# Seven block products in place of eight at 31 places of the down products, and a ring of eight weight slots in place of ten

## What is computed

```python
def second_block(x, attn_norm, w_in, ..., w_o, mlp_norm, w_up, w_down, final_norm):
    for l in range(DEPTH):
        h = rms_norm_2(x, attn_norm[l])
        proj = h @ w_in[l]
        ...
        x = x + mixed @ w_o[l]
        h = rms_norm_2(x, mlp_norm[l])
        x = x + jnp.square(jax.nn.relu(h @ w_up[l])) @ w_down[l]
    return rms_norm_2(x, final_norm)
```

## Time and profile before

| | |
|---|---|
| runs | 2908.87, 2910.0 and 5743.55 us, median 2910.0 |
| profiled execution, time | 2908.11 us |
| its span | 2906.3 us |
| mean granted TensorE clock | 0.994 |
| TensorE busy with matmuls | 2826.6 us, 14616 matmuls |
| VectorE busy | 1895.0 us |
| ScalarE busy | 1439.6 us |
| moved by DMA | 611.88 MB, mean 211 GB/s |

### The profile page before, as it was taken

One profiled execution on the slowest core, in us unless ns is written; L12 is line 12 of the kernel. 1 busy time (PEld: TensorE's weight loads), 2 busy tenths in 40 slices (PEclk: granted clock), 3 DMA queues, 4 the chain that ended last, 5 costly groups with the idle time before them and its releaser, 6 DMA issues.

```text
span 2906.3 us, 36886 instructions
## 1 busy us (share of the span) xinstructions
PE 2826.6 (97%) x14616; PEld 2440.8 (84%) x14616; DVE 1895.0 (65%) x2401; ACT 1439.6 (50%) x2029; POOL 39.0 (1%) x48
## 2 busy tenths in 40 slices
PE   5998998999999999999999999999999999999998
PEld 5887787898889888888888888898888888888887
DVE  7999998679854566655445554545666654456554
ACT  5455544565546554644334444555546443344443
POOL 0000000000000000000000000000000000000000
PEclk9999999999999999999999999999999999999999
DMA  9996598767655455556665566564545556655653
GB/s 392 363 361 225 195 370 301 248 201 259 240 170 185 150 174 163 177 189 191 194 194 188 189 192 193 180 186 153 171 164 176 191 191 195 193 186 191 206 195 138
DMA packets 173882, 611.88 MB, mean 211 GB/s; under 512 B 19680, under 2 KB 19952, under 8 KB 173072
## 3 DMA queue, kind: packets, MB, share of 16 engines
q1 hardware_dynamic: 170912, 600.42, 61.4%
q0 software_dynamic: 1824, 6.61, 0.8%
q10 hardware_dynamic: 976, 2.51, 0.3%
HBM read 607.34 MB, written 2.11 MB: 210 GB/s over the span
## 4 chain that ended last, share of the span: by engine, by line
PE 86%; DVE 7%; ACT 2%; DMA 2%; issue 1%; SPq 0%; POOL 0%; POOLq 0%; ACTq 0%; DVEq 0%
PE ps L2025 19%; PE ps L2028 19%; PE ps L2032 18%; PE ps L2044 16%; PE ps L2054 8%; DVE w_lo L1260 2%; PE ps L1971 2%; DVE raw L1416 2%; PE ps L2252 1%; DMA raw<-in_w_ina 1%; PE ps L2231 1%; ACT w_hi L883 1%; DMA raw<-in_w_modT 1%; DVE proj L1390 1%; DMA raw<-in_w_in 0%
## 5 line engine op out<-in xcount | busy, mean ns | idle before, releaser
L1260 DVE TENSOR_TENSOR w_lo<-raw,w_hi 128x1024 fp32r<-128x1024 f32 (+4 forms) x988 | 1149.8, 1175 | 865.1 <-ACT w_hi L883 862.0
L883 ACT ACTIVATE w_hi<-raw 128x1024 fp32r<-128x1024 f32 (+4 forms) x988 | 994.5, 1018 | 1168.7 <-PE ps L2032 642.9
L2025 PE MATMUL ps<-w_hi,hT_both 128*128 128x512 f32 (+3 forms) x1824 | 478.9, 384 | 15.9 <-DVE proj L1390 8.1
L2044 PE MATMUL ps<-hT_both,w_hi 128*128 128x512 f32 x2048 | 490.2, 391 | 0.9 <-DVE u L1364 0.9
L2028 PE MATMUL ps<-w_lo,hT_both 128*128 128x512 f32 (+3 forms) x1824 | 462.2, 375 | 0.6 <-DVE w_lo L1260 0.6
L2032 PE MATMUL ps<-w_hi,hT_both 128*128 128x512 f32 (+3 forms) x1824 | 459.3, 373 | 0.0
L2044 PEld LDWEIGHTS ps<-hT_both,w_hi 128*128 128x128 f32 x2048 | 376.1, 188 | 74.1 <-DVE u L1364 1.3
L2028 PEld LDWEIGHTS ps<-w_lo,hT_both 128*128 128x128 f32 x1824 | 339.7, 189 | 50.8 <-DVE w_lo L1260 1.9
L2025 PEld LDWEIGHTS ps<-w_hi,hT_both 128*128 128x128 f32 x1824 | 326.9, 189 | 63.0 <-DVE proj L1390 12.2
L2032 PEld LDWEIGHTS ps<-w_hi,hT_both 128*128 128x128 f32 x1824 | 339.1, 188 | 48.4
L2025 PE MATMUL ps<-w_hi,uT_hi 128*128 128x512 f32 x1024 | 275.1, 390 | 0.0
(11 more groups left out here) (256 smaller groups left out, 1549.7 us busy)
## 6 DMA issues: line engine op xcount, KB each, us to landing
raw<-in_w_up SPq DMA_DIRECT2D x256, 512.0 KB, 3.8
raw<-in_w_down SPq DMA_DIRECT2D x256, 512.0 KB, 4.2
raw<-in_w_modT SPq DMA_DIRECT2D x192, 512.0 KB, 5.8
raw<-in_w_rest SPq DMA_DIRECT2D x80, 456.0 KB, 3.5
raw<-in_w_z SPq DMA_DIRECT2D x64, 512.0 KB, 4.4
raw<-in_w_out SPq DMA_DIRECT2D x64, 512.0 KB, 4.4
raw<-in_w_rest SPq DMA_DIRECT2D x48, 344.0 KB, 3.4
raw<-in_w_oa SPq DMA_DIRECT2D x32, 512.0 KB, 3.4
```

What stands on the lines that cost most here:

```text
L883: act.activation(hi_blocks(L % SPLIT_SLOTS, c, w), blocks(raw, G % RAW_SLOTS, c, w), ACT.Copy).then_inc(S.hi_ready, 1)
L1260: dve.tensor_tensor(blocks(w_lo, r, c, w), blocks(raw, r, c, w), hi_blocks(s, c, w).bitcast(F32), ALU.subtract).then_inc(S.group_read, 1)
L2025: pe.matmul(o, rows(hi, c, t), wh[:, c], start=start and c == 0, stop=False)
L2044: pe.matmul(ps[:, bank(job, i, f)], wh[:, c, f * P:(f + 1) * P], hT_both[:, k0 + c].rearrange("p a n -> p (a n)"), start=k0 + c == 0, stop ...
```

## The change

A pair of column tiles of a down job is now taken together (`joined` pairs of tiles: two in down00, down01 and down10, one in down11), with the steps of the two tiles alternating. At the groups in `QUADS` (2, 5, 8, 11 for the first half, 2, 4, 6, 8, 10 for the second) the two groups hold a matrix of 2 x 2 weight blocks (two chunks, two tiles), and u holds 2 x 2 blocks (two tokens' blocks, two chunks). Their product is made with seven block products and not eight, after Winograd's form of Strassen's scheme. It needs four sums of left blocks, made and split when the up tile is (`sums`), and three combinations of right blocks, made from the raw weights (`combine`, then `combos_hi` and `combos_lo`). Three of the seven go to three of the four banks of the pair's tiles (`c11`, `c12`, `c21` in the code), four to banks 4 to 7, where they add up over the quads of a pair; `take_parts` then adds them to x. There are 8 + 10 + 8 + 5 = 31 such quads. TensorE does nothing in the first step of a quad and 21 matmuls in the second.

The ring has eight slots and not ten; its place is used for the sums and combinations. The turned blocks for `c21` come at other steps, and the final norm's row is loaded later, since the tiles that they need end in another order.

```diff
-RAW_SLOTS = 10
+RAW_SLOTS = 8
+QUADS = ((2, 5, 8, 11), (2, 4, 6, 8, 10))
...
     def steps(self):
         tiles, groups = range(self.tiles), range(len(self.groups))
+        if self.joined:
+            return ([(2 * p + a, j) for p in range(self.joined) for j in groups for a in range(2)]
+                    + [(i, j) for i in tiles[2 * self.joined:] for j in groups])
...
-                    product(f"down{l}{h}", (uT_hi, uT_lo), evac="dve", tail=TAIL if l == DEPTH - 1 and h else 0))])]
+                    product(f"down{l}{h}", (uT_hi, uT_lo), evac="dve", tail=TAIL if l == DEPTH - 1 and h else 0,
+                            joined=1 if l == DEPTH - 1 and h else 2, quads=QUADS[h]))])]
...
-        lead("c21", *after("c21", -8, -7, -6, -5, -4, -3, 3, 4))
+        lead("c21", *after("c21", -4, -3, -2, -1, 1, 2, 3, 4))
...
-            pool.wait_ge(S.group_multiplied, jobs["down11"].L)
+            pool.wait_ge(S.group_multiplied, jobs["down11"].L + 2 * len(jobs["down11"].groups))
...
+                if job.seven(i, j) and i % 2:
+                    act.wait_ge(S.combined, 4 * quad_of(i, L) + 2)
                 act.wait_ge(raw_landed[G % RAW_SLOTS], 16 * (G // RAW_SLOTS + 1))
...
+                    act.activation(combos_hi[h][:], combos[h][:], ACT.Copy).then_inc(S.combos_rounded, 1)
...
+            def combine(job, i, L):
+                h, q = int(job.name[-1]), quad_of(i, L)
+                e = combos[h]
+                first, second = (blocks(raw, group_at[L + a] % RAW_SLOTS, 2, COLS) for a in range(2))
+                b11, b21, b12, b22 = first[:, 0], first[:, 1], second[:, 0], second[:, 1]
...
+                if q:
+                    dve.wait_ge(S.combos_multiplied, q)
...
+                dve.tensor_tensor(e[:, 0], b22, b12, ALU.subtract).then_inc(S.combined, 1)
...
+                dve.tensor_tensor(b12, b12, b11, ALU.subtract).then_inc(S.combined, 1)
...
+                dve.tensor_tensor(e[:, 1], b22, b12, ALU.subtract).then_inc(S.combined, 1)
...
+                dve.tensor_tensor(e[:, 2], b21, e[:, 1], ALU.subtract).then_inc(S.combined, 1)
...
+                a11, a12, a21, a22 = v[:, 0, 0:P], v[:, 1, 0:P], v[:, 0, P:2 * P], v[:, 1, P:2 * P]
+                dve.tensor_tensor(to[:, 2], a11, a21, ALU.subtract).then_inc(S.sums_ready, 1)
+                dve.tensor_tensor(to[:, 0], a21, a22, ALU.add).then_inc(S.sums_ready, 1)
...
+                dve.tensor_tensor(to[:, 1], to[:, 0], a11, ALU.subtract).then_inc(S.sums_ready, 1)
...
+                dve.tensor_tensor(to[:, 3], a12, to[:, 1], ALU.subtract).then_inc(S.sums_ready, 1)
...
+            def seven_products(job, p, j, L):
...
+                plain = [(ps[:, 4], left(0, 0), hi0[:, 0], lo0[:, 0], True), (c11, left(1, 0), hi0[:, 1], lo0[:, 1], False),
+                         (c12, total(3), hi1[:, 1], lo1[:, 1], False), (ps[:, 5], total(0), hi1[:, 0], lo1[:, 0], True)]
+                mixed = [(o, a, combos_hi[h][:, k], combos_lo[h][:, k], own)
+                         for k, (o, a, own) in enumerate(((ps[:, 7], total(2), True), (ps[:, 6], total(1), True), (c21, left(1, 1), False)))]
...
+                mm.then_inc(S.group_multiplied, 2)
+                pe.wait_ge(S.combos_rounded, q + 1)
...
+                pe.wait_ge(S.combos_split, q + 1)
...
+                mm.then_inc(S.combos_multiplied, 1)
```

More of the change, by code:

```diff
@@ L206, in steps, with together, seven, after_quads @@
         return [(i, j) for j in groups for i in tiles] if self.swept else [(i, j) for i in tiles for j in groups]
+    def together(self, i):
+        return i < 2 * self.joined
+    def seven(self, i, j):
+        return self.together(i) and j in self.quads
+    def after_quads(self, i, j):
+        return 2 * (j - max(self.quads) - 1) + i % 2 if self.together(i) else -1
     def in_tail(self, i, j):
@@ L559, in up_tiles, with quad_of, last_quad, sums_of @@
             return ups.index(job) * job.tiles + i + 1
+        downs = [jobs[f"down{l}{h}"] for l in range(DEPTH) for h in range(2)]
+        summed = {(job.layer, int(job.name[-1]), j): k
+                  for k, (job, j) in enumerate((job, j) for job in downs for j in job.quads)}
+        quad_at = {L: k for k, L in enumerate(L for job in downs for q, (i, j) in enumerate(job.steps())
+                                              for L in (job.L + q,) if i % 2 and job.seven(i, j))}
+        superpairs = {(job.name, p): k for k, (job, p) in enumerate((job, p) for job in downs for p in range(job.joined))}
+        def quad_of(i, L):
+            return quad_at[L if i % 2 else L + 1]
+        def last_quad(job, p):
+            return quad_at[job.L + job.steps().index((2 * p + 1, max(job.quads)))]
+        def sums_of(job, i):
+            down = jobs["down" + job.name[-2:]]
+            return down.quads.index(i) if i in down.quads else None
         def ahead(jobs_):
@@ L566, in ahead @@
                 end = min(q + AHEAD + 1, len(groups))
-                yield (*group, [(job, j, L) for job, i, j, L in groups[upto:end]])
+                yield (*group, groups[upto:end])
                 upto = end
@@ L1070, in wide @@
                         out_squares(job, i - 1)
-                    if i and j == 3 and job.kind == "down" and job.name[-1] == "1":
-                        squares_of(job, i - 1, junk_m[:])
+                    if job.joined and job.after_quads(i, j) == 1:
+                        copy_part(job, i // 2)
+                    if i >= 2 and i % 2 == 0 and j == 3 and job.name == "down01":
+                        for done in range(2):
+                            squares_of(job, done, junk_m[:])
+                    if i >= 2 and j == 3 and job.name == "down11":
+                        for done in range(2) if i == 2 else (2,):
+                            squares_of(job, done, junk_m[:])
                     if j == last:
@@ L1223, in _ @@
                 else:
-                    squares_of(jobs[f"down{l - 1}1"], 3, probs2[:, 0])
+                    for done in (2, 3):
+                        squares_of(jobs[f"down{l - 1}1"], done, probs2[:, 0])
                 walk.upto(c2.L + 18)
@@ L1254, in link, with lo @@
                 dve.wait_ge(S.dve_step, n(S.dve_step))
-            def lo(job, j, L):
+            def lo(job, i, j, L):
+                if job.seven(i, j) and i % 2 == 0:
+                    combine(job, i, L)
                 dve.wait_ge(S.hi_ready, L + 1)
@@ L1391, in evacuate @@
                     return
+                if job.kind == "down" and job.together(i):
+                    dve.wait_ge(S.part_added, 4 * (superpairs[job.name, i // 2] + 1))
                 for t in range(TOK):
@@ L1455, in wide @@
                 prev = None
+                ended = []
                 for job, i, j, L, splits in ahead(order):
@@ L1458, in wide @@
                         tail(job, j - len(job.groups) + TOK)
+                    if ended and ended[0][2] <= L:
+                        evacuate(*ended.pop(0)[0:2])
                     if prev and prev[0].kind in ("inb", "inc", "ind") and j == 1:
```

142 lines of the change are left out of this document (137 added, 5 removed).

## The result

The changed kernel takes 2940.3 us (2938.64 to 2944.43), the kernel before in the same comparison 2909.43 us. The ratio is 1.0111, with a 95% interval from 1.0094 to 1.0129. So it is 31 us slower, where 6 us faster was forecast, and outside the range of 2889 to 2917. That is under 2%, but the interval lies wholly above 1. The profiled execution took 2939.47 us. One profiled execution of a later kernel (z0's loads spread evenly at ten slots) took 3081.2 us at a mean granted clock of 0.865, where its other four took 2895 to 2897, and no reading rests on it.

A forecast was written before the change was run, and what follows sets the result against it. TensorE's matmuls plus its pauses were taken to bound the kernel. 2908.1 - 21.1 (matmuls) + 2.6 (bank waits) + 12.7 (fewer slots) = 2902.3 us; with 1.9 from profiled execution to median, 2904 us, range 2889 to 2917.

The forecast's parts named there:

- A saved matmul: Down products: each of 93 matmuls saved was to be worth its pitch of 0.2267 us, together 21.1 us.
- the fourth rival: Matmuls saved in the down products are worth only 131 ns each, giving 2913 us; chance 0.02.
- The wait of a down product's second group: Each of four down products: TensorE waits 0.65 us for VectorE to finish with a bank, +2.6 us in all.
- The combinations are hidden: Dense quads: VectorE's combinations fit behind 10.2 us of matmuls, 0.65 and 1.4 us to spare, cost 0 us.
- The third rival: Combinations come late in the dense quads, 1 us of wait at twelve quads, giving 2916 us; chance 0.08.
- the next tile finds its bank drained: End of a pair in down products: evacuation takes 1.5 us, TensorE's group between 2.72, so no wait was expected.
- the sum's ring term: First network's four stretches: eight load slots for ten were to cost 12.7 us in all.
- z0.: Stretch z0: loads for steps 6 to 13 wait for the product three groups back, +2.5 us (0 to 28).
- in1.: Stretch in1: later loads for groups 7, 10, 13 and 16 were to cost +7.7 us (3 to 11).
- ina to ind.: Stretch ina to ind: one group later, +2.44 us, mostly cancelled by shorter queueing, -2.6; +2 us taken (0 to 41).
- The second rival: Fewer slots cost more than the saved matmuls give, mainly in z0 and ina to ind: 2921 us; chance 0.18.
- The first rival: Fewer slots cost nothing, since queueing shrinks by just what is lost: 2891.5 us; chance 0.2.

## Why the prediction was wrong

**What held.** A saved matmul is worth 0.2267 us and the down products are TensorE's throughout (24 matmuls again: +21.1), so the fourth rival is out. The wait of a down product's second group for the bank that `square_u` drains came as forecast, in one place per job:

```profile
1403.54 1.07 PE L2205 MATMUL ps<-w_hi,uT_lo 128*128 128x512 f32 x4
1405.11 1.20 PE L2198 MATMUL ps<-w_hi,uT_hi 128*128 128x512 f32 x4 [0.50 <-DVE u L1503]
```

The packs of four are spaced 0.91 us, so the product before ended at 1404.45 and the pause is 0.66 us, for 0.65 forecast. The combinations are hidden. At a dense quad of down01 (VectorE, then TensorE):

```profile
1788.67 0.69 DVE L1373 TENSOR_TENSOR combos<-raw,combos 128x512 f32<-128x512 f32 x1
...
1791.68 1.75 DVE L1352 TENSOR_TENSOR combos_lo<-combos,combos_hi 128x1536 fp32r<-128x1536 f32 x1
...
1794.97 0.61 PE L2251 MATMUL ps<-combos_lo,sums_hi 128*128 128x512 f32 x2
```

Their low part is ready at 1793.43, 1.5 us ahead of its matmul; 1.4 was the forecast. The third rival is out. The 1.8 us that the down products gave less lie mostly at the end of down01, where c21's first group finds its bank occupied. The prediction had priced this at nothing ("the next tile finds its bank drained"):

```profile
1920.62 1.09 PE L2198 MATMUL ps<-w_hi,hT_both 128*128 128x456 f32 x4 [1.10 <-DVE x L1496]
```

A joined pair ends both tiles together, so the last but one is drained later than when tiles ended sixteen groups apart.

**The step that failed** is the sum's ring term, 12.7 us for a measured 47.8, and within it three sentences.

*z0.* "But a group's product comes two long steps after its split, and VectorE has other work: of 0 to 9 x 3.1 = 28 us I take +2.5." It cost 16.2. The prediction followed the late load to its own product, which does come two steps later, and gave it that slack. But ScalarE and VectorE work through their lists in order. The rounding and the split that wait for the load stand ahead of attention work for an earlier step, and the product just before needs that. The loop is product L - 3, load L, product L - 1. The turn shown above takes 12.0 us and brings two products, 6.0 us each; with the release four back the same turn would bring three, 4.0 us each. Measured over those eight steps are 7.2 us a step at three back (changed kernel), 5.3 at four (kernel before), 5.0 at four to five (spread evenly, eight slots). In pairs, as a turn brings them, steps 7 to 14 took 12.0, 12.5, 13.6 and 19.7 us, for 9.4, 10.7, 10.7 and 11.6 before. So every turn loses, as the distance of the release has it, but over half of the loss in these steps is in the last, at step 13. There the load of step 15, released by the product of step 12, holds the list of ScalarE ahead of attention work (`probsT`):

```profile
303.56 5.38 DMA raw<-in_w_z
...
309.93 0.59 ACT probsT L1172
...
310.56 3.67 PE ps L2475 x16
```

TensorE stood still for 6.2 us (0.7 at the same place before), and the sixteen matmuls behind that took 3.67 us for 2.00. The rule of one turn gives the direction of the loss and not its size.

*in1.* The sum there was 2.7 and 2.2 us for two loads and 1.4 each for two others, 7.7 us. The loop was seen, the load of group 10 was issued at 525.31 with the product of group 7 as forecast, and the sign was right. The size was 19.4, and two causes can be named. The first is the start. In the kernel before, the load of group 5 was issued at 454.23, ahead of TensorE's long pause before in1, and in the changed kernel it waits out the pause:

```profile
483.95 16.90 SPq L860 DMA_DIRECT2D raw<-in_w_modT  x2
503.24 0.33 SPq L860 DMA_DIRECT2D raw<-in_w_in  x1
```

It lands at 506.77, and group 6 then comes 8.0 us after group 5, 5.2 more than its own length. The rows are SyncE's; the first covers two `W_mod` loads, the second of which went out behind the pause. In the plan the release of group 5's load moves across the pause, from out0's last product to in1's second, and the prediction looked at groups 7, 10, 13 and 16 only. The run with 14 `W_mod` loads in in1 has this release back at out0's last product and all the later ones four or more back; in1 was 22 us shorter in it. Group 6 still took 5.2 us there, so the release of group 5's load is not shown to be the whole of its growth. The second cause is the later pauses. The groups behind one, 9, 12 and 15, took 7.6, 10.1 and 8.3 us for 4.7, 4.6 and 6.5 before, and group 18, for which the sum had nothing, took 6.3 for 2.7. Part of both is that TensorE ran slower behind the pauses, for which the sum had no term either: by the busy times above that is 6.9 of the 19.4 us. Group 9 grew by 2.9 us for 2.7 forecast, and that is luck. The load of 4.75 us in the earlier trace rows was not without a queue ahead, as the prediction has it: two `W_mod` loads issued at 486.19 were still under way. In the changed kernel it took 3.52 us, 1.2 less, and twelve matmuls behind the pause that took 4.26 us in place of 2.72 took this back.

*ina to ind.* "Most of it cancels": two loads fewer in the queue were to give back 2.6 us of 2.44. By the trace a group's load took 6.62 us from issue to landing before and 5.51 after (means over inb to ind), so 1.1 us came back. The loads ahead in the queue were released late themselves. ScalarE starts the rounding 0.02 us after the landing in some 40 of 48 groups, 35 before. The stretch lost 10.6 us for 2. That it is this difference which makes the whole 10.6 was not tried by itself. Nor is the 10.6 firm: in the six kernels with eight slots throughout the stretch took 219.5 to 224.3 us, in the five with ten 209.9 to 213.1.

The second rival had the right places ("z0 and ina to ind, where VectorE has almost no idle time") and 2921 us, with a chance of 0.18. It fell short of the 47.8 us above all in z0 (9 for 16.2) and in1 (11 for 19.4). The first rival (2891.5) is near the kernel with ten slots, then eight: 2895.37.

## What to carry to other kernels

A ring of buffers that serves loads, rounding and splitting in strict order can close a loop. As a first guess (it gave the direction here and not the size), its pace is its turn's length divided by the products between release and blocked product; one step less in three is then a third of the pace, not one load. Count for each load how many products back its release lies, and ask who stands behind the waiting instruction on its engine, not when its own data is used. Where memory is wanted in one phase only, give it back in that phase only: the same edit was +31 us with the eight slots throughout and -14 us with ten in the first network.

## What the runs showed of the hardware

TensorE behind a pause, in1 of the changed kernel:

```profile
535.95 1.07 PE L2198 MATMUL ps<-w_hi,hT_both 128*128 128x512 f32 x4
...
546.87 2.04 PE L2198 MATMUL ps<-w_hi,hT_both 128*128 128x512 f32 x4 [4.83 <-ACT hT_both L1024]
548.71 1.91 PE L2201 MATMUL ps<-w_lo,hT_both 128*128 128x512 f32 x4
550.42 1.75 PE L2205 MATMUL ps<-w_hi,hT_both 128*128 128x512 f32 x4
552.00 1.09 PE L2198 MATMUL ps<-w_hi,hT_both 128*128 128x512 f32 x4
```

and the windows over the second to fourth of these rows and over what follows:

```profile
546.90:552.00 5.10, 5.10 (x12) 3.99 (x13) 5.10 (x7) 1.84 (x2) 0.00 (x0) 0.52 0.27 111
552.00:558.00 6.00, 6.00 (x29) 4.71 (x27) 1.50 (x4) 0.00 (x0) 0.00 (x0) 1.00 0.79 259
```

Twelve matmuls took 5.13 us in place of 2.72, at a granted clock of 0.52, which is the lower of the two levels (1.2 GHz for 2.4). Then the clock was 1.00 again. TensorE had stood still for 4.83 us before. In the kernel before, the pause ahead of the product at 496.52 us, which the earlier trace rows show in the chain, was shorter, and the packs behind it kept their spacing of about 0.91 us. Behind the third pause of the same kernel, hardly longer, they did not:

```profile
496.52 1.16 PE L2025 MATMUL ps<-w_hi,hT_both 128*128 128x512 f32 x4 [1.70 <-ACT hT_both L952]
497.51 1.07 PE L2028 MATMUL ps<-w_lo,hT_both 128*128 128x512 f32 x4
498.42 1.07 PE L2032 MATMUL ps<-w_hi,hT_both 128*128 128x512 f32 x4
...
517.92 1.97 PE L2025 MATMUL ps<-w_hi,hT_both 128*128 128x512 f32 x4 [1.95 <-ACT hT_both L952]
519.69 1.88 PE L2028 MATMUL ps<-w_lo,hT_both 128*128 128x512 f32 x4
```

So slow matmuls also stand behind a pause of 1.95 us, and the length of the pause alone does not say whether they come. A pause that the ring makes can cost more than its own length: TensorE's busy time differs by 15 us between the changed kernel and the one with ten slots first, with the same instructions. The load of 512 KB at 265.46 us, with no load queued ahead of it, landed 3.52 us after its issue.
